# A float32r matmul kernel whose weight slabs are interleaved column by column, so that the stationary operand is read with a step of two

## The reference, cut to what matters

```
p = x @ w_in                                             # (512 or 768) x 1024 times 1024 x n
h = causal_depthwise_conv(x @ w_up, conv_w, conv_b)      # 1024 -> 5632
(jax.nn.silu(gate) * val) @ w_down                       # 2816 -> 1024
jnp.concatenate([ya, yb], axis=-1) @ w_out
```

## Time and profile before

| | |
|---|---|
| median of 3 runs | 2966.07 us (2965.58 to 2967.16) |
| span of the profiled execution | 2965.5 us |
| PE busy | 2901.6 us, 98%, 15438 matmuls |
| PEld busy | 2393.2 us, 81%, 15438 loads |
| DVE busy | 1477.4 us, 50% |
| ACT busy | 1163.9 us, 39% |
| HBM traffic | 250.50 MB read, 86 GB/s over the span |

### The profile page before, as it was taken

The page is one execution under the profiler, slowest core; times in us unless marked ns, Lnnn a source line. Parts: engine busy times, 40 slices in busy tenths (PEclk is TensorE's granted clock), DMA queues, the critical chain, the costliest instruction groups (busy, mean ns, idle before and its releaser), DMA issues.

```text
span 2965.5 us, 38348 instructions
## 1 busy us (share of the span) xinstructions
PE 2901.6 (98%) x15438; PEld 2393.2 (81%) x15438; DVE 1477.4 (50%) x2051; ACT 1163.9 (39%) x1856; POOL 146.0 (5%) x199
## 2 busy tenths in 40 slices
PE   9999999999999999999999999999999999999998
PEld 7778888776788887877888788868888788888776
DVE  5655455546463657366252543263455735453454
ACT  5444333526452344146233431173232743341452
POOL 1000000110000000100000300100001000200100
PEclk9999999999999999999999999999999999999999
DMA  5343332331332222210112221311113022321322
GB/s 185 122 158 105 113 128 85 129 130 38 136 107 98 99 87 76 82 54 22 60 43 76 85 68 57 101 60 64 57 64 101 21 82 78 108 91 66 121 75 85
DMA packets 48844, 260.98 MB, mean 88 GB/s; under 512 B 6872, under 2 KB 7904, under 8 KB 24896
## 3 DMA queue, kind: packets, MB, share of 16 engines
q1 hardware_dynamic: 36288, 213.75, 20.8%
q0 software_dynamic: 12416, 45.25, 4.5%
HBM read 250.50 MB, written 4.28 MB: 86 GB/s over the span
## 4 chain that ended last, share of the span: by engine, by line
PE 91%; DVE 4%; ACT 3%; DMA 1%; issue 1%; POOL 0%; SPq 0%; DVEq 0%; ACTq 0%
PE PS L897 15%; PE PS L898 15%; PE PS L899 15%; PE PS L874 7%; PE PS L876 7%; PE PS L875 7%; PE PS L833 3%; PE PS L835 3%; PE PS L834 3%; PE PS L1124 2%; PE PS L1086 1%; PE PS L1197 1%; PE PS L1179 1%; PE PS L1166 1%; PE PS L944 1%
## 5 line engine op out<-in xcount | busy, mean ns | idle before, releaser
L897 PE MATMUL PS<-HHX,WHX 128*128 128x512 f32 (+1 forms) x1440 | 504.6, 350 | 0.4 <-DVE WLX L2409 0.3
L898 PE MATMUL PS<-HL,WHX 128*128 128x512 f32 (+1 forms) x1440 | 503.4, 350 | 0.0
L1680 ACT ACTIVATE WHX<-W 128x2048 fp32r<-128x2048 f32 (+1 forms) x102 | 174.8, 1713 | 560.9 <-DMA W<-in_w 379.2
L899 PE MATMUL PS<-HHX,WLX 128*128 128x512 f32 (+1 forms) x1008 | 350.1, 347 | 0.0
L2409 DVE TENSOR_TENSOR WLX<-W,WHX 128x2048 fp32r<-128x2048 f32 x60 | 137.5, 2292 | 344.9 <-ACT WHX L1680 344.8
L897 PEld LDWEIGHTS PS<-HHX,WHX 128*128 128x128 f32 x1440 | 272.7, 189 | 38.3 <-DVE WLX L2409 1.5
L898 PEld LDWEIGHTS PS<-HL,WHX 128*128 128x128 f32 x1440 | 272.7, 189 | 34.9
L874 PE MATMUL PS<-HH,WH 128*128 128x512 f32 x672 | 261.7, 389 | 0.0
L876 PE MATMUL PS<-HH,WL 128*128 128x512 f32 x672 | 261.7, 389 | 0.0
L875 PE MATMUL PS<-HL,WH 128*128 128x512 f32 x672 | 261.6, 389 | 0.0
L2409 DVE TENSOR_TENSOR WL<-W,WH 128x2048 fp32r<-128x2048 f32 x68 | 155.7, 2290 | 177.8 <-ACT WH L1680 177.7
(11 more groups left out here) (553 smaller groups left out, 5813.8 us busy)
## 6 DMA issues: line engine op xcount, KB each, us to landing
W<-in_w SPq DMA_DIRECT2D x172, 1024.0 KB, 4.8
XC<-in_wm POOLq DMA_DIRECT2D x12, 1024.0 KB, 5.2
H<-in_wm POOLq DMA_DIRECT2D x12, 1024.0 KB, 6.0
W<-in_wb SPq DMA_DIRECT2D x24, 512.0 KB, 3.3
W<-in_w SPq DMA_DIRECT2D x8, 768.0 KB, 4.1
ARENA<-ARENA POOLq DMA_DIRECT2D x32, 128.0 KB, 2.3
ARENA<-mrow SPq DMA_DIRECT2D x12, 256.0 KB, 3.9
PR<-in_nbias POOLq DMA_DIRECT2D x12, 256.0 KB, 3.0
```

The costliest lines, as they stand in the source:

```text
L897: pe.matmul(dst, wh[:, s, c], hi[:, k, t0:t1], start=k == 0, stop=False)
L898: pe.matmul(dst, wh[:, s, c], lo[:, k, t0:t1], start=False, stop=False)
L899: mm = pe.matmul(dst, wl[:, s, c], hi[:, k, t0:t1], start=False, stop=k == kb - 1)
L1680: act.activation(dst[:, s, 0:n], W[:, s, 0:n], ACT.Copy).then_inc(wh_ready[s], 1)
```

## The change

The host writes the two 128-column blocks of a tile k interleaved: column 0 of m = 0, column 0 of m = 1, column 1 of m = 0, and so on. A block is then every second number of a stretch of 256, and `paired(i)` (i = 2k + m) names it. The slabs of `w_mod` keep their order, and so do those of `pe_tok`, which another function lays out. DMAs, the split on ACT and DVE, and all other reads stay as they are, since the split works on whole slabs without regard to the order of columns. Each engine has the same instructions in the same order as before; what differs is the access pattern of the stationary operand.

```diff
+    def paired(i):
+
+        first = i // 2 * SLAB + i % 2
+        return slice(first, i // 2 * SLAB + SLAB, 2)
+
...
-                hi, lo = (v[:, k % 4, m * P:(m + 1) * P] for v in halves[k // 4])
+                hi, lo = (v[:, k % 4, paired(m)] for v in halves[k // 4])
...
-                        c = slice(k * SLAB + m * P, k * SLAB + m * P + P)
+                        c = paired(2 * k + m)
                         pe.matmul(dst, wh[:, s, c], hi[:, k, t0:t1], start=k == 0, stop=False)
                         pe.matmul(dst, wh[:, s, c], lo[:, k, t0:t1], start=False, stop=False)
                         mm = pe.matmul(dst, wl[:, s, c], hi[:, k, t0:t1], start=False, stop=k == kb - 1)
...
-                c = slice(k * SLAB, k * SLAB + P)
+                c = paired(2 * k)
...
-    def slabs(w, cols):
+    def slabs(w, cols, paired=True):
 
-        return [w[:, c:c + SLAB].reshape(-1, P, SLAB).transpose(1, 0, 2).reshape(P, -1) for c in cols]
+        tiles = [w[:, c:c + SLAB].reshape(-1, P, SLAB // P, P) for c in cols]
+        return [(v.transpose(1, 0, 3, 2) if paired else v.transpose(1, 0, 2, 3)).reshape(P, -1) for v in tiles]
...
-    wm = [slab for l in range(LAYERS) for slab in slabs(a["w_mod_2"][l], range(0, 3 * D, SLAB))]
+    wm = [slab for l in range(LAYERS) for slab in slabs(a["w_mod_2"][l], range(0, 3 * D, SLAB), False)]
```

More of the change, by code:

```diff
@@ L610, in pe_head_high @@
         for k in ks:
-            hi = halves[k // 4][0][:, k % 4, m * P:(m + 1) * P]
+            hi = halves[k // 4][0][:, k % 4, paired(m)]
             pe.matmul(PS[:, m, :], hi, HHX[:, k, 0:T], start=k == 0, stop=False)
@@ L620, in pe_head_low @@
         for k in range(KT):
-            mm = pe.matmul(PS[:, m, :], halves[k // 4][1][:, k % 4, m * P:(m + 1) * P], HHX[:, k, 0:T],
+            mm = pe.matmul(PS[:, m, :], halves[k // 4][1][:, k % 4, paired(m)], HHX[:, k, 0:T],
                            start=False, stop=k == KT - 1)
```

## The result

The changed kernel takes 3023.93 us (median of 4 runs, 3022.68 to 3026.47) beside 2965.89 us for the kernel before on the same chip. The ratio is 1.0195, 95% interval 1.0181 to 1.0210. The change makes the kernel 58 us slower; I had forecast no change.

What follows compares the result with a forecast made beforehand. The prediction took PE's stream of matmuls (98% busy) as the bound. Unchanged parts cost 0 and the stepped stationary read 0, so 2965.5 + 0 = 2965.5 us, a median forecast of 2966 us, range 2848 to 3110 us.

Steps and rivals of the forecast that it cites:

- The bound: Whole kernel: PE busy 2901.6 of 2965.5 us, 98%, so the time follows the distance between matmuls almost one to one.
- Parts that cost nothing: Instructions, order, semaphores, DMAs, layout before launch, and the split on ACT and DVE: unchanged by the change, cost 0.
- No price: Stationary reads with a step of two: 9.6 bytes per ns, the moving read's rate already, so 0 us added; chance 0.50.
- fixed constant of 13.3 ns: Every float32r matmul: 0.417 ns per moving column plus 13.3 ns, the same under 512 and 256 columns.
- The range: Whole kernel, to hold 8 in 10: from the gain at 2848 us to the nearer slowdown at 3110 us.
- None under the 256-column ones: A slower load has 106 ns of room under 512-column matmuls, but none, after the 13 ns constant, under 256-column ones.
- the doubled load: Rival: stepped load takes 213 ns, not 107; 2304 matmuls of 256 columns go from 120 to 227 ns, +246 us; chance 0.10.
- The constant goes: Rival: the step parts colliding load and moving read, 11 ns off each of 10656 matmuls, -117 us, 2849 us; chance 0.22.
- the four rows: Plain fp32 records of 256 columns, read as four matmuls with a stationary operand each, 213 ns apart, nothing left over.
- The contrast: The 13.3 ns constant shows for float32r but hardly for plain fp32, whose moving read runs at half the rate.
- The same collision, doubled: Rival: twice the fetches take twice the moving read's slots, 13.3 to 26.6 ns on 10656 matmuls, +142 us; chance 0.14.

## Why the prediction was wrong

**The bound** was right: the time is the stream of matmuls, 8352 distances are 6.9 ns longer in the mean, 58 us, and the span is 55.5 us longer.

**Parts that cost nothing** (split, DMAs, order, layout) were right but for at most some 5 us: the step without the layout gives +47 us on 7500 matmuls, and +6 us for the other 852 leaves 5 of the 58 us without a shown cause.

**The step that failed is "No price".** I compared rates: the load with a step of two passes over memory as fast as the moving read does, so nothing forbids it. The rate is indeed nearly held (118 ns per load beside 111 where it is the bound). But the price under 512 columns, 6.7 ns for each of 8352 matmuls where I had put 0, does not come from the rate: a contiguous load from another address costs as much. It depends on where and in what pattern the two operands are read; that the two reads get in each other's way is my reading of that. I had treated the distance of 226.7 ns as columns plus a fixed constant of 13.3 ns. It is the lowest mean of many, which reach from 226.7 to 238 in the rows shown, and it is tied to how contiguous blocks lie against the moving tile. A step, a shift of one of the two by 4 to 192 bytes, and fewer stationary columns all lie above it.

**The range** that I worked out, 2848 to 3110 us, holds the measured 3024, but by luck: it went up to 3110 for a collision of 13.3 ns on all 10656 matmuls, and neither the size nor the widths are those measured.

**"None under the 256-column ones" was wrong as well**: I expected these to be touched first, since a load uses 107 of their 120 ns. At step two a load needs 118 ns in its own train, which still fits into 120; at step four it doesn't, and there my sum for the doubled load held (112 ns for each of 2112 matmuls, where I had 107 for each of 2304). The mechanism of that rival is real, but it needs a larger step than two.

**The rivals.** "The constant goes" is refuted: the step made the distance longer, no form under 512 columns had a mean under 226.7 ns, and loads of 64 and 32 columns, with a half and a quarter of the fetches, made it longer too. One of its supports was misread, too: a plain fp32 matmul leaves two records (the 64 of line 106 gave 128), so the four rows were two matmuls, not four with an operand each. The 8 matmuls of line 860 with their 16 rows could have told me. The contrast itself holds: (55.09 - 0.59)/127 = 429.1 ns between two such records of 512 columns is 2 x 213.3 + 2.5 ns. "The same collision, doubled" is the nearest: it named the two reads and the right lines, put 13.3 ns on all 10656 matmuls, and got half of that on 8352 of them. It was wrong that the cost follows the number of fetches: step four costs 9.4 ns, step two 6.3, step two from another address 3.9 (29 us over 7500), and a contiguous read 32 bytes off 6.4.

**A row that I could have read.** In the kernel before, lines 968 to 970 read contiguous blocks that start 72 columns, 288 bytes, apart. Its timeline there, 23 matmuls from first to last:

```profile
585.76 0.40 PE L969 MATMUL PS<-HL,WFH 128*128 128x512 f32 x1
...
590.86 0.40 PE L970 MATMUL PS<-HHO,WFL 128*128 128x512 f32 x1
```

22 distances in 5.10 us are 231.8 ns, in the same trace in which the other lines of this form have a median distance of 226 or 227 ns. 288 bytes are 32 more than 256, so most of these blocks lie off the favourable distance. That contradicted a fixed constant before any experiment.

**What stays open**: which memory or engine resource makes 256 bytes a period (the shift of both by 16 bytes, and 128 against 384 bytes, show that this isn't the whole rule), why 384 moving columns show no addition at all while 512 do, neither by the step nor by 32 bytes (11.28 us), and the last 5 us of the changed kernel. The runs show the dependence on addresses and width, not the circuit behind it. That the pattern of the load as such (its longer record of 195 ns) shifts the two reads out of step in the changed kernel is the reading that fits all runs, but only the distances were measured, not the reads.

## What to carry to other kernels

Where a kernel is one long stream of float32r matmuls of 512 columns, keep the stationary blocks contiguous and a multiple of 256 bytes away from the moving tiles, and shift both, if at all, by 32 bytes or 64 and not by 16: 1.6% of this kernel hung on it, and a shift of 32 bytes costs as much as a step of two. Before a cost is called fixed, look for the one line in the trace whose operands lie differently and compare its distance. Measure distances between starts, in trains of one form: the loads' records moved by 7 ns here and said nothing on which width would pay.

## What was not expected of the hardware

- The distance of float32r matmuls with 512 columns depends on the addresses of the two operands: 226.7 ns at a shift of 0 or 256 bytes, 229 to 238 when one of them is shifted by 4 to 192 (kernel: 2967.08 us at 256 bytes, 3014.30 at 32).
- Fewer stationary columns made a matmul dearer: 226.7 ns with 128, 230 with 64, 232 with 32.
- A step of two in the stationary operand leaves the load at 118 ns against 111, a step of four doubles it: 233 to 235 ns whatever the moving width.
- One load with a step among three slows all three distances: 230.9, 230.0 and 232.4 ns where they were 226.7.
- A step of two under 384 float32r columns, and one of two or four under 512 plain fp32 columns, cost nothing: 173.3 ns beside 173.5, and 55.10 us beside 55.09 for a train.
